# The opening of a decoder step: two groups in turn, first chunk in halves, squares of x on ACT

## The chip, the cores and the metric

The kernel runs on one NeuronCore of a Trainium2 chip. What counts is the device time of one execution in microseconds. PE is TensorE, DVE is VectorE, ACT is ScalarE, POOL is GpSimd, SP is SyncE, whose queue here only issues DMAs. All times below are microseconds from the start of the span unless marked otherwise.

## What is computed

One layer of a hybrid decoder for 256 prompt tokens and 8 decode tokens (264 columns in all), in f32:

```python
h = rms_norm(x, g_pre_mix)                       # D_MODEL = 2048
z = h @ w_in                                     # 17 groups of 256 columns
qa, ka, va, qb, kb, vb = split(z)                # rope on the first 16 of 64 dims of q and k
o_a = sink_normalise(banded(qa, ka, va, 128))    # 16 heads over 2 kv heads
o_b = merge(dilated(qb, kb, vb, w, d) for w, d in ((128, 1), (512, 4), (2048, 16)))
x += rms_norm(concat(rms_norm(o_a), rms_norm(o_b)) @ w_out, g_post_mix)
h = rms_norm(x, g_pre_ffn)                       # D_FF = 5632
y = (gelu(dwconv3(h @ w_gate)) * (h @ w_up)) @ w_down
x += rms_norm(y, g_post_ffn)
```

## The kernel before

All matrices are streamed as chunks of 128x1024 f32 (512 KB, `CH`) through a ring of four slots (`RING`). Chunk n goes through five hands: SP loads it into `raw` as soon as DVE has finished with the chunk four before it (`lo_ready`); ACT casts it to fp32r, `wh` (L390, `hi_ready`); DVE subtracts, `wl = raw - wh` (L627, `lo_ready`); PE multiplies (`gemm`, `weights_used`). A product is three matmuls of 264 columns, `wh*hh`, `wh*hl` and `wl*hh` (L1061 to L1063, `mm3`), where `hh` and `hl` are the high and low parts of x times its gain. A chunk holds four k-tiles of 128 rows by 256 columns, so it is 4 x 2 x 3 = 24 matmuls. A group of 256 output columns of `w_in` takes four chunks, one for each quarter of x; groups alternate between PSUM banks 0, 1 and 2, 3.

The opening: SP issues the small part of `par` (gains), then x in four quarters (4 k-tiles, 528 KB each) alternating with the four chunks of group 0, then the rest of `par`, `ident`, `tab` (masks and cosines, 808 KB), and from chunk 4 on one chunk for each that DVE frees. ACT makes four `hh` (L520) per quarter of x and one cast; DVE makes the `hl` (L786), with its weight operations among them; POOL squares x in four operations of 128x1056 into `xsq` (L999).

After that the order of each engine is a table, `PLAN`: `PLAN[n]` lists the stages that follow chunk n. Each engine walks it in the same way, so DVE and ACT work on their part of the stage behind their operation on chunk n+2 or n+3. The stages that matter here are "ss" (PE sums the squares, L1081), "ss2" (PE sums over partitions, L1100; ACT takes the root, L403; DVE the reciprocal `rB`, L695, and multiplies the cosine tables by it), "evac" of a group (DVE rotates and scales PSUM into q, k or v), "vtr" and "vdec" (PE transposes v), "S" (scores, L1134 and L1136), "R" (DVE scales the exponentials) and "T" (PE transposes them). The row norm 1/rms is applied only at evacuation, so group 0 can be multiplied before it is known, but not evacuated.

Of the kernel before, what the change touches and what calls it, by code (L numbers as in the profile page):

```python
# [178 lines left out]
def build(nc, d):  # L179

    ctx = ExitStack()
    with ctx:
# [158 lines left out]
        def _(sp):  # L341
# [8 lines left out]
            sp.dma_start(xT[:, 0:4], d["x"][:, 0:4]).then_inc(x_landed[0], 16)  # L350
            load(chunk(0, 0, 4, 0), d["w_in"][GROUPS[0][2], 0])
            for c in range(1, 4):
                sp.dma_start(xT[:, 4 * c:4 * c + 4], d["x"][:, 4 * c:4 * c + 4]).then_inc(x_landed[c], 16)
                load(chunk(0, 0, 4, c), d["w_in"][GROUPS[0][2], c])
# [1 line left out]
            sp.dma_start(ident[:], d["ident"]).then_inc(tab_landed, 16)
            sp.dma_start(tab[:], d["tab"]).then_inc(tab_landed, 16)
            for n in range(4, N_IN):
                load(chunk(n, 0, 4, 0), d["w_in"][GROUPS[n // 4][2], n % 4])
# [21 lines left out]
        def _(act):  # L381
# [133 lines left out]
            line.do(nc.scalar.activation(small[:, 100:101], eps[:], ACT.Copy))  # L515
            act.wait_ge(gains_landed, 16)
            for j in range(MT):
                if j % 4 == 0:
                    act.wait_ge(x_landed[j // 4], 16)
                nc.scalar.activation(hh[:, j], xT[:, j], ACT.Copy,  # L520
                                     scale=par[:, C_GPM + j:C_GPM + j + 1]).then_inc(xh_ready, 1)
                if j in (3, 7, 11):
                    split(chunk(0, 0, 4, j // 4))
# [95 lines left out]
        def _(dve):  # L619
# [163 lines left out]
            for j in range(MT):  # L783
# [4 lines left out]
                if j in (3, 7):  # L788
                    split(chunk(0, 0, 4, j // 4))
# [689 lines left out]
```

## Time and profile before

| | us |
|---|---|
| median of 3 runs | 1202.35 (1202.26 to 1202.55) |
| the profiled execution | 1202.52 |
| its span | 1200.7 |
| mean granted clock of TensorE | 0.992 |
| PE busy | 1164.7 (97%) |
| DVE busy | 704.1 (59%) |
| ACT busy | 551.3 (46%) |
| POOL busy | 115.2 (10%) |

A row of a timeline reads: start, duration, engine, line, operation, output and inputs, shapes, count, and in brackets how long the engine was idle before it and what ended that. Durations of matmuls overlap, so for PE the distance from start to start is what one costs. The span begins 1.8 us short of the whole time; the difference lies around it.

### The profile page before, as it was taken

To read this page: it belongs to the slowest core of one execution; us is meant where nothing else is said; L and a number is where in the kernel's file an instruction comes from. 1 tells how busy PE (TensorE), PEld (TensorE's weight loads), DVE (VectorE), ACT (ScalarE), POOL (GpSimd) and SP (SyncE) were. 2 spreads that over 40 slices of the span, in tenths; PEclk is the share of its full clock that TensorE was granted. 3 is DMA by queue.
4 is the path that set the end of the run, shared out by engine and by line. 5 is a ranking of instruction groups with operands and counts; after the bars stand their busy time and mean duration, and the time that the engine had idled before them with its cause. 6 is when DMAs were issued, how large, how long until landed. Compare 5 with 4: busy or idle time off the path is not lost.

```text
span 1200.7 us, 25500 instructions
## 1 busy us (share of the span) xinstructions
PE 1164.7 (97%) x9921; PEld 1132.3 (94%) x9921; DVE 704.1 (59%) x1049; ACT 551.3 (46%) x855; POOL 115.2 (10%) x167
## 2 busy tenths in 40 slices
PE   5999999999999799999999999999999999999995
PEld 4999898989899799999999999999999999999995
DVE  6786665576475866656565655656565444454445
ACT  5445555565455654445344444444444433343331
POOL 3100111111002001001001100100010000020001
PEclk9999999999999899999999999999999999999998
DMA  7555786777556346464555555554555655555551
GB/s 290 172 174 158 257 245 231 232 226 249 183 159 179 116 136 202 158 208 160 190 166 184 179 170 194 173 190 156 196 170 193 193 179 185 176 178 184 181 157 73
DMA packets 59042, 222.21 MB, mean 185 GB/s; under 512 B 7017, under 2 KB 7217, under 8 KB 56881
## 3 DMA queue, kind: packets, MB, share of 16 engines
q1 hardware_dynamic: 54720, 196.58, 50.4%
q0 software_dynamic: 4272, 24.94, 6.3%
q8 instruction: 35, 0.57, 0.2%
q14 instruction: 15, 0.11, 0.0%
HBM read 216.45 MB, written 5.00 MB: 184 GB/s over the span
## 4 chain that ended last, share of the span: by engine, by line
PE 93%; DVE 4%; DMA 1%; ACT 1%; issue 0%; POOL 0%; SPq 0%; DVEq 0%; ACTq 0%
PE ps L1061 29%; PE ps L1062 29%; PE ps L1063 29%; DVE hl L786 1%; PE ps L1227 1%; PE ps L1145 1%; DMA Vk<-in_vb 1%; DVE wl L627 1%; PE ps L1208 1%; PE ps L1136 1%; PE ps L1134 1%; PE ps L1163 0%; PE ps L1081 0%; DVE yT L905 0%; DMA xT<-in_x 0%
## 5 line engine op out<-in xcount | busy, mean ns | idle before, releaser
L1061 PE MATMUL ps<-hh,wh 128*128 128x264 f32 x2080 | 601.2, 289 | 19.2 <-DVE wl L627 13.5
L1063 PE MATMUL ps<-hh,wl 128*128 128x264 f32 x2080 | 594.2, 286 | 0.0
L1062 PE MATMUL ps<-hl,wh 128*128 128x264 f32 x1952 | 558.8, 286 | 0.0
L627 DVE TENSOR_TENSOR wl<-raw,wh 128x1024 fp32r<-128x1024 f32 x364 | 439.4, 1224 | 187.7 <-ACT wh L390 187.3
L390 ACT CAST wh<-raw 128x1024 fp32r<-128x1024 f32 x364 | 375.7, 1045 | 282.7 <-PE ps L1063 272.0
L1061 PEld LDWEIGHTS ps<-hh,wh 128*128 128x128 f32 x2080 | 395.1, 190 | 31.3 <-issue 16.9
L1063 PEld LDWEIGHTS ps<-hh,wl 128*128 128x128 f32 x2080 | 394.1, 189 | 0.0
L1062 PEld LDWEIGHTS ps<-hl,wh 128*128 128x128 f32 x1952 | 369.8, 189 | 0.1
L1062 PE MATMUL ps<-gl,wh 128*128 (+1 forms) x704 | 200.4, 285 | 0.0
L1061 PE MATMUL ps<-gh,wh 128*128 (+1 forms) x704 | 200.1, 284 | 0.0
L1063 PE MATMUL ps<-gh,wl 128*128 (+1 forms) x704 | 199.5, 283 | 0.0
L1061 PEld LDWEIGHTS ps<-gh,wh 128*128 128x128 f32 x704 | 132.5, 188 | 0.9 <-issue 0.9
L1062 PEld LDWEIGHTS ps<-gl,wh 128*128 128x128 f32 x704 | 132.6, 188 | 0.0
L1063 PEld LDWEIGHTS ps<-gh,wl 128*128 128x128 f32 x704 | 132.4, 188 | 0.0
L1027 POOL COPY co<-U 128x4 f32 (+1 forms) x22 | 21.2, 964 | 423.4 <-DVE U L841 423.4
L840 DVE TENSOR_TENSOR U<-ps,rB 128x512 f32<-128x512 f32 x22 | 15.2, 691 | 73.2 <-PE ps L1063 73.2
L865 DVE TENSOR_TENSOR up<-ps,rB 128x528 f32<-128x528 f32 x21 | 14.9, 707 | 67.8 <-PE ps L1063 67.8
L576 ACT ACTIVATE cv<-U,par 128x280 f32<-128x280 f32 x44 | 25.0, 617 | 63.5 <-DVE U L841 63.5
L586 ACT CAST gh<-up 128x528 f32 (+1 forms) x22 | 14.0, 634 | 73.0 <-DVE up L868 72.9
L850 DVE SCALAR_TENSOR_TENSOR cv<-U,par,cv 128x280 f32<-128x280 f32 x88 | 41.0, 506 | 9.9 <-ACT cv L576 6.9
L1061 PE MATMUL ps<-oBh,wh 128*128 128x264 f32 x128 | 37.6, 294 | 0.0
L1062 PE MATMUL ps<-hh,wh 128*128 128x264 f32 x128 | 36.5, 285 | 0.0
(224 smaller groups left out, 830.7 us busy)
## 6 DMA issues: line engine op xcount, KB each, us to landing
raw<-in_w_gate SPq DMA_DIRECT2D x88, 512.0 KB, 3.7
raw<-in_w_up SPq DMA_DIRECT2D x88, 512.0 KB, 4.6
raw<-in_w_down SPq DMA_DIRECT2D x88, 512.0 KB, 4.3
raw<-in_w_in SPq DMA_DIRECT2D x68, 512.0 KB, 4.8
raw<-in_w_out SPq DMA_DIRECT2D x32, 512.0 KB, 3.8
Kt<-in_kb POOLq DMA_DIRECT2D x8, 1284.0 KB, 6.2
Vk<-in_vb POOLq DMA_DIRECT2D x8, 1024.0 KB, 7.5
xT<-in_x SPq DMA_DIRECT2D x4, 528.0 KB, 6.6
```

The lines of the kernel that those rows point to most:

```text
L390: nc.scalar.copy(wh[:, slot], raw[:, slot]).then_inc(hi_ready, 1)
L576: nc.scalar.activation(cv[:, k], U[:, k, 0:NU - 2], ACT.Identity, scale=par[:, bass.ds(i * 2 + (C_CW + k), 1)], bias=par[:, bass.ds(i * 2 ...
L586: nc.scalar.copy(gh[:, bass.ds(i * 2, 2)], up[:]).then_inc(gh_ready, 1)
L627: V.tensor_tensor(wl[:, slot], raw[:, slot], wh[:, slot].bitcast(F32), ALU.subtract).then_inc(lo_ready, 1)
L786: V.scalar_tensor_tensor(hl[:, j], xT[:, j], par[:, C_GPM + j:C_GPM + j + 1], hh[:, j].bitcast(F32), ALU.mult, ALU.subtract).then_inc(xl_r ...
L840: line.do(V.tensor_tensor(U[:, :, 2:2 + SEQ], ps[:, g:g + 2, 0:SEQ], wide(rB[:, 0:SEQ]), ALU.mult))
L850: ins = V.scalar_tensor_tensor(cv[:, k], U[:, k, tap:tap + NU - 2], par[:, bass.ds(i * 2 + (C_CW + FT * tap + k), 1)], cv[:, k], ALU.mult, ...
L865: V.tensor_tensor(up[:], ps[:, 2:4, 0:TOK], wide(rB[:]), ALU.mult).then_inc(up_taken, 1)
L1027: line.do(G.tensor_copy(co[:, bass.ds(i * 2, 2), 0:2], U[:, :, SEQ:SEQ + 2]))
L1061: nc.tensor.matmul(out, a, x, start=start, stop=False)
L1062: nc.tensor.matmul(out, a, xl, start=False, stop=False)
L1063: return nc.tensor.matmul(out, b, x, start=False, stop=stop)
```

## The change

Nothing but the first ten chunks and what stands between them is written differently.

- Order of chunks: groups 0 and 1 are multiplied in turn, a quarter of x at a time (`part_in`): chunk 0 is group 0 quarter 0, chunk 1 group 1 quarter 0, chunk 2 group 0 quarter 1, and so on. Group 0 ends with chunk 6, group 1 with chunk 7.
- The first chunk and the first quarter of x are loaded in halves; the first chunk is cast and subtracted in halves too (`half_landed`, `half_hi`, `half_lo`).
- `xsq` is made by ACT with Square (in four operations), not by POOL. ACT loads the Sqrt table at the start.
- `hl` of x is made by DVE just ahead of the quarter that needs it.
- "ss" stands at chunk 4 (was 2), "ss2" at 5 (3), "evac" of group 0 at 7 (4), of group 1 at 8 (8), "vtr" at 8 (5), "vdec" at 9 (6), "aload" (loads of cache A by POOL) at 9 (8). All later stages keep their places.
- The cosine tables are loaded after chunk 5, `ident` and the masks after chunk 7, the rest of `par` after chunk 9. The sinks stand in the first part of `par`.
- In the evacuation of group 0 the value product comes before the second rotation product and signals `kv_taken`; the first matmul of group 2 waits for it.
- PE multiplies `ones` by `ones` 13 times (128x128, f32) at the start, into a bank that is not yet used.

```diff
-C_SINK = C_ST + FT * 16
-T_MA, T_MB, T_COS, T_SIN, T_MD = 0, 384, 768, 768 + TOK, 768 + 2 * TOK
+T_COS, T_SIN, T_MA, T_MB, T_MD = 0, TOK, 2 * TOK, 2 * TOK + 384, 2 * TOK + 768
+FIRST = 8
+WARM = 13
+X_PARTS = ((0, 2), (2, 4), (4, 8), (8, 12), (12, 16))
+def part_in(n):
+    return (n % 2, n // 2) if n < FIRST else (n // 4, n % 4)
 def group_end(gi):
+    if gi < 2:
+        return FIRST - 1 + gi
...
-    add(2, "ss")
-    add(3, "ss2")
+    add(4, "ss")
+    add(5, "ss2")
...
             sp.dma_start(par[:, 0:C_CW], d["par"][:, 0:C_CW]).then_inc(gains_landed, 16)
...
+            load_x(0)
+            sp.dma_start(raw[:, 0, 0:CH // 2], w0[:, 0:CH // 2]).then_inc(half_landed, 16)
+            load_x(1)
+            sp.dma_start(raw[:, 0, CH // 2:CH], w0[:, CH // 2:CH]).then_inc(raw_landed[0], 16)
+            load_in(1)
+            load_x(2)
+            load_in(2)
+            load_x(3)
+            load_in(3)
+            load_x(4)
+            load_in(4)
+            load_in(5)
+            sp.dma_start(tab[:, 0:2 * TOK], d["tab"][:, 0:2 * TOK]).then_inc(angles_landed, 16)
+            load_in(6)
+            load_in(7)
+            sp.dma_start(ident[:], d["ident"]).then_inc(tab_landed, 16)
+            sp.dma_start(tab[:, 2 * TOK:], d["tab"][:, 2 * TOK:]).then_inc(tab_landed, 16)
+            load_in(8)
+            load_in(9)
             sp.dma_start(par[:, C_CW:], d["par"][:, C_CW:]).then_inc(par_landed, 16)
...
-            line.do(nc.scalar.activation(small[:, 100:101], eps[:], ACT.Copy))
+            line.do(nc.scalar.activation(small[:, 100:101], eps[:], ACT.Sqrt))
...
+            high(0)
+            act.wait_ge(half_landed, 16)
+            nc.scalar.copy(wh[:, 0, 0:CH // 2], raw[:, 0, 0:CH // 2]).then_inc(half_hi, 1)
+            high(1)
+            act.wait_ge(raw_landed[0], 16)
+            nc.scalar.copy(wh[:, 0, CH // 2:CH], raw[:, 0, CH // 2:CH]).then_inc(hi_ready, 1)
+            split(chunk(0, 0, 4, 1))
+            high(2)
+            split(chunk(0, 0, 4, 2))
+            square_x(0)
+            square_x(1)
             for n in range(N_ATT):
                 split(chunk(0, 0, 4, n + 3))
+                if n == 0:
+                    high(3)
+                    square_x(2)
+                elif n == 1:
+                    high(4)
+                    square_x(3)
...
-                line.step(V.stream_shuffle(sh[:, 0:n], src, SWAP))
+                line.do(V.stream_shuffle(sh[:, 0:n], src, SWAP))
+                if n == 1:
+                    V.tensor_tensor(vT[:, 0], ps[:, 1, 0:TOK], rB[:], ALU.mult).then_inc(kv_taken, 1)
+                line.need(line.n)
...
-            for c in range(4):
-                pool.wait_ge(x_landed[c], 16)
-                G.tensor_tensor(xsq[:, 4 * c:4 * c + 4], xT[:, 4 * c:4 * c + 4], xT[:, 4 * c:4 * c + 4],
-                                ALU.mult).then_inc(xsq_ready, 1)
...
+            pe.wait_ge(const_ready, 2)
+            for k in range(WARM):
+                nc.tensor.matmul(ps[:, 6, 0:P], ones[:], ones[:], start=True, stop=True)
             for n in range(N_ATT):
                 if n < N_IN:
-                    gi, c = n // 4, n % 4
-                    if c == 0 and gi >= 2:
+                    gi, c = part_in(n)
+                    if c == 0 and gi == 2:
+                        pe.wait_ge(kv_taken, 1)
+                    elif c == 0 and gi > 2:
                         pe.wait_ge(evac_done, gi - 1)
                     gemm(chunk(0, 0, 4, n), 2 * (gi % 2), hh, hl, 4 * c, c == 0, c == 3,
-                         xl_ready if gi == 0 else None)
+                         xl_ready if gi < 2 else None)
```

DVE at the start of the program, before (L786 makes a low part of x, L627 one of weights; "x3" means three alike in a row):

```order
L786 SCALAR_TENSOR_TENSOR hl<-xT,par,hh 128x264 [waits xh_ready,gains_landed]
L786 SCALAR_TENSOR_TENSOR hl<-xT,par,hh 128x264 [waits xh_ready] x3
L627 TENSOR_TENSOR wl<-raw,wh 128x1024 [waits hi_ready]
L786 SCALAR_TENSOR_TENSOR hl<-xT,par,hh 128x264 [waits xh_ready] x4
L627 TENSOR_TENSOR wl<-raw,wh 128x1024 [waits hi_ready]
L786 SCALAR_TENSOR_TENSOR hl<-xT,par,hh 128x264 [waits xh_ready] x8
L627 TENSOR_TENSOR wl<-raw,wh 128x1024 [waits hi_ready] x4
```

The same place of DVE now (L844 the low parts of x, L849 and L853 the halves of chunk 0, L681 the later chunks):

```order
L844 SCALAR_TENSOR_TENSOR hl<-xT,par,hh 128x264 [waits xh_ready]
L849 TENSOR_TENSOR wl<-raw,wh 128x512 [waits half_hi]
L844 SCALAR_TENSOR_TENSOR hl<-xT,par,hh 128x264 [waits xh_ready] x2
L853 TENSOR_TENSOR wl<-raw,wh 128x512 [waits hi_ready]
L681 TENSOR_TENSOR wl<-raw,wh 128x1024 [waits hi_ready]
L844 SCALAR_TENSOR_TENSOR hl<-xT,par,hh 128x264 [waits xh_ready] x4
L681 TENSOR_TENSOR wl<-raw,wh 128x1024 [waits hi_ready] x2
L844 SCALAR_TENSOR_TENSOR hl<-xT,par,hh 128x264 [waits xh_ready] x4
L681 TENSOR_TENSOR wl<-raw,wh 128x1024 [waits hi_ready]
L844 SCALAR_TENSOR_TENSOR hl<-xT,par,hh 128x264 [waits xh_ready] x4
L681 TENSOR_TENSOR wl<-raw,wh 128x1024 [waits hi_ready] x3
```

The low parts of the third and fourth quarter of x, which stood ahead of chunk 2's weights, now stand behind those of chunks 3 and 4.

ACT now, from the second half of chunk 0 (L566) to chunk 5 (L555 a high part of x, L559 a square, L424 a cast of weights):

```order
L566 CAST wh<-raw 128x512 [waits raw_landed0]
L424 CAST wh<-raw 128x1024 [waits raw_landed1]
L555 ACTIVATE hh<-xT,par 128x264 [waits x_landed2]
L555 ACTIVATE hh<-xT,par 128x264 x3
L424 CAST wh<-raw 128x1024 [waits raw_landed2]
L559 ACTIVATE xsq<-xT 128x1056 x2
L424 CAST wh<-raw 128x1024 [waits raw_landed3]
L555 ACTIVATE hh<-xT,par 128x264 [waits x_landed3]
L555 ACTIVATE hh<-xT,par 128x264 x3
L559 ACTIVATE xsq<-xT 128x1056
L424 CAST wh<-raw 128x1024 [waits weights_used,raw_landed0]
```

Before, ACT had only high parts and casts there; the squares are new on it.

DVE around the reciprocal and the first evacuation, before (L694 to L698 the reciprocal and its tables, L636 to L652 rotation and value product of group 0):

```order
L694 TENSOR_SCALAR small<-par 128x17 [waits tab_landed,par_landed,misc_ready,misc_free]
L695 RECIPROCAL rB<-rms 128x264
L697 TENSOR_TENSOR tab<-tab,rB 128x264 [waits dve_line]
L698 TENSOR_TENSOR tab<-tab,rB 128x264
L627 TENSOR_TENSOR wl<-raw,wh 128x1024 [waits hi_ready,dve_line]
L636 SCALAR_TENSOR_TENSOR r<-ps,tab 128x264 [waits weights_used]
L637 STREAM_SHUFFLE sh<-ps 128x264
L638 SCALAR_TENSOR_TENSOR sh<-sh,tab 128x264 [waits dve_line]
L639 TENSOR_TENSOR kA<-r,sh 128x264 [waits dve_line]
L652 TENSOR_TENSOR vT<-ps,rB 128x264 [waits dve_line]
```

And now:

```order
L749 TENSOR_SCALAR small<-par 128x17 [waits angles_landed,misc_ready,misc_free]
L750 RECIPROCAL rB<-rms 128x264
L752 TENSOR_TENSOR tab<-tab,rB 128x264 [waits dve_line]
L753 TENSOR_TENSOR tab<-tab,rB 128x264
L681 TENSOR_TENSOR wl<-raw,wh 128x1024 [waits hi_ready,dve_line]
L681 TENSOR_TENSOR wl<-raw,wh 128x1024 [waits hi_ready]
L690 SCALAR_TENSOR_TENSOR r<-ps,tab 128x264 [waits weights_used]
L691 STREAM_SHUFFLE sh<-ps 128x264
L693 TENSOR_TENSOR vT<-ps,rB 128x264
L695 SCALAR_TENSOR_TENSOR sh<-sh,tab 128x264 [waits dve_line]
L696 TENSOR_TENSOR kA<-r,sh 128x264 [waits dve_line]
```

Two weight operations now stand between the tables and the evacuation, where one stood, and the value product has moved up behind the shuffle.

## Rows read from the trace of the kernel before

**Rows 1.** The page's chain that ended last, share of the span by engine.

```profile
PE 93%; DVE 4%; DMA 1%; ACT 1%; issue 0%; POOL 0%; SPq 0%; DVEq 0%; ACTq 0%
```

**Rows 2.** Waits of PE, whole span: us in total, times, longest.

```profile
PE ps L1061 <- DVE wl L627: 13.5, 3, 11.8
```

**Rows 3.** Timeline of PE: start, duration, line, [idle before and its cause].

```profile
11.82 0.59 PE L1061 MATMUL ps<-hh,wh 128*128 128x264 f32 x1 [11.82 <-DVE wl L627]
...
17.05 0.42 PE L1063 MATMUL ps<-hh,wl 128*128 128x264 f32 x1
17.95 0.39 PE L1061 MATMUL ps<-hh,wh 128*128 128x264 f32 x1 [0.48 <-DVE wl L627]
...
22.32 0.39 PE L1061 MATMUL ps<-hh,wh 128*128 128x264 f32 x1 [1.18 <-DVE wl L627]
...
25.44 1.99 PE L1081 MATMUL ps<-xsq,ones 128*32 128x264 f32 x32
...
38.85 0.44 PE L1115 MATMUL ps<-ident,vT 128*128 128x128 f32 x2 [1.97 <-DVE kdup L656]
...
42.08 0.37 PE L1061 MATMUL ps<-hh,wh 128*128 128x264 f32 x1
...
50.84 0.29 PE L1063 MATMUL ps<-hh,wl 128*128 128x264 f32 x1
51.05 0.49 PE L1134 MATMUL ps<-kdup,qs 64*128 64x128 f32 x4
...
403.94 0.56 PE L1061 MATMUL ps<-hh,wh 128*128 128x264 f32 x1 [5.75 <-DVE hl L814]
```

**Rows 4.** Timeline of DVE from 6 to 21 us, pieces of several windows.

```profile
6.07 4.56 DVE L786 SCALAR_TENSOR_TENSOR hl<-xT,par,hh 128x264 fp32r<-128x264 f32 x4 [5.02 <-ACT hh L520]
...
11.69 2.17 DVE L786 SCALAR_TENSOR_TENSOR hl<-xT,par,hh 128x264 fp32r<-128x264 f32 x1
...
15.88 0.88 DVE L786 SCALAR_TENSOR_TENSOR hl<-xT,par,hh 128x264 fp32r<-128x264 f32 x2
...
17.82 3.31 DVE L786 SCALAR_TENSOR_TENSOR hl<-xT,par,hh 128x264 fp32r<-128x264 f32 x8
```

**Rows 5.** Timeline of POOL: the first square, the third, third and fourth together.

```profile
5.41 1.95 POOL L999 TENSOR_TENSOR xsq<-xT 128x1056 f32<-128x1056 f32 x1 [4.07 <-DMA xT<-in_x]
...
10.55 3.03 POOL L999 TENSOR_TENSOR xsq<-xT 128x1056 f32<-128x1056 f32 x1 [0.61 <-DMA xT<-in_x]
...
10.55 5.12 POOL L999 TENSOR_TENSOR xsq<-xT 128x1056 f32<-128x1056 f32 x2 [0.61 <-DMA xT<-in_x]
```

**Rows 6.** ACT's groups by line: count | busy us, mean ns | idle before.

```profile
L390 ACT CAST wh<-raw 128x1024 fp32r<-128x1024 f32 x364 | 375.7, 1045 | 282.7 <-PE ps L1063 272.0 <-DMA raw<-in_w_in 9.9 <-ACT ge L596 0.3
...
L495 ACT ACTIVATE sq<-oT 128x1056 f32<-128x1056 f32 x4 | 4.3, 1084 | 0.1
```

**Rows 7.** The chain in order of time: start, us, what.

```profile
1.20 4.14 DMA xT<-in_x
...
51.12 0.42 PE ps L1134 x4
```

**Rows 8.** The page's DMA issues: count, KB each, us to landing (0 to 60 us).

```profile
par<-in_par SPq DMA_DIRECT2D x1, 40.0 KB, 1.8
```

**Rows 9.** Windows: engines busy (count), granted clock, DMA share, GB/s; the second PE alone.

```profile
20.00:25.00 5.00, 3.82 (x32) 3.61 (x31) 5.00 (x7) 1.04 (x1) 0.00 (x0) 1.00 0.42 136
...
405.00:410.00 5.00, 5.00 (x25) 0.51 0.28 81
```

**Rows 10.** Timeline of DVE: start and end of the reciprocal block, and of an evacuation.

```profile
31.55 0.17 DVE L694 TENSOR_SCALAR small<-par 128x17 f32<-128x17 f32 x1 [5.88 <-ACT rms L403]
...
34.28 1.22 DVE L627 TENSOR_TENSOR wl<-raw,wh 128x1024 fp32r<-128x1024 f32 x1
...
45.29 0.71 DVE L636 SCALAR_TENSOR_TENSOR r<-ps,tab 128x528 f32<-128x528 f32 x1 [0.47 <-PE ps L1063]
...
48.75 1.23 DVE L627 TENSOR_TENSOR wl<-raw,wh 128x1024 fp32r<-128x1024 f32 x1
```

More of the change, by code:

```diff
@@ L349, in _, with load_x, load_in @@
             sp.dma_start(par[:, 0:C_CW], d["par"][:, 0:C_CW]).then_inc(gains_landed, 16)
[L350 to L354, printed above, removed]
+            def load_x(c):
+                k0, k1 = X_PARTS[c]
+                sp.dma_start(xT[:, k0:k1], d["x"][:, k0:k1]).then_inc(x_landed[c], 16)
+            def load_in(n):
+                g, c = part_in(n)
+                load(chunk(n, 0, 4, 0), d["w_in"][GROUPS[g][2], c])
+            w0 = d["w_in"][GROUPS[0][2], 0]
+            load_x(0)
[17 more added lines that the diff above has]
+            load_in(9)
             sp.dma_start(par[:, C_CW:], d["par"][:, C_CW:]).then_inc(par_landed, 16)
[L356 to L359, printed above, removed]
+            for n in range(10, N_IN):
+                load_in(n)
             with sp.Fori(0, (N_OUTA + N_OUTB) // 4) as i:
@@ L514, in _, with high, square_x @@
             act.wait_ge(const_ready, 1)
-            line.do(nc.scalar.activation(small[:, 100:101], eps[:], ACT.Copy))
+            line.do(nc.scalar.activation(small[:, 100:101], eps[:], ACT.Sqrt))
             act.wait_ge(gains_landed, 16)
[L517 to L523, printed above, removed]
+            def high(c):
+                act.wait_ge(x_landed[c], 16)
+                for j in range(*X_PARTS[c]):
+                    nc.scalar.activation(hh[:, j], xT[:, j], ACT.Copy,
+                                         scale=par[:, C_GPM + j:C_GPM + j + 1]).then_inc(xh_ready, 1)
+            def square_x(q):
+                nc.scalar.activation(xsq[:, 4 * q:4 * q + 4], xT[:, 4 * q:4 * q + 4], ACT.Square).then_inc(xsq_ready, 1)
+            high(0)
[9 more added lines that the diff above has]
+            square_x(1)
             for n in range(N_ATT):
                 split(chunk(0, 0, 4, n + 3))
+                if n == 0:
[4 more added lines that the diff above has]
+                    square_x(3)
                 for s in PLAN[n]:
@@ L782, in _, with low_x @@
             dve.wait_ge(gains_landed, 16)
-            for j in range(MT):
-                dve.wait_ge(xh_ready, j + 1)
-                V.scalar_tensor_tensor(hl[:, j], xT[:, j], par[:, C_GPM + j:C_GPM + j + 1],
-                                       hh[:, j].bitcast(F32), ALU.mult, ALU.subtract).then_inc(xl_ready, 1)
-                if j in (3, 7):
-                    split(chunk(0, 0, 4, j // 4))
+            def low_x(c):
+                for j in range(*X_PARTS[c]):
+                    dve.wait_ge(xh_ready, j + 1)
+                    V.scalar_tensor_tensor(hl[:, j], xT[:, j], par[:, C_GPM + j:C_GPM + j + 1],
+                                           hh[:, j].bitcast(F32), ALU.mult, ALU.subtract).then_inc(xl_ready, 1)
+            low_x(0)
+            dve.wait_ge(half_hi, 1)
+            V.tensor_tensor(wl[:, 0, 0:CH // 2], raw[:, 0, 0:CH // 2], wh[:, 0, 0:CH // 2].bitcast(F32),
+                            ALU.subtract).then_inc(half_lo, 1)
+            low_x(1)
+            dve.wait_ge(hi_ready, 1)
+            V.tensor_tensor(wl[:, 0, CH // 2:CH], raw[:, 0, CH // 2:CH], wh[:, 0, CH // 2:CH].bitcast(F32),
+                            ALU.subtract).then_inc(lo_ready, 1)
+            split(chunk(0, 0, 4, 1))
+            low_x(2)
             for n in range(N_ATT):
                 split(chunk(0, 0, 4, n + 2))
+                if n == 1:
+                    low_x(3)
+                elif n == 2:
+                    low_x(4)
                 for s in PLAN[n]:
@@ L1071, in gemm @@
                         pe.wait_ge(split, kt0 + k + 1)
+                    if isinstance(n, int) and n == 0 and k == 2:
+                        pe.wait_ge(lo_ready, 1)
                     for m in range(2):
```

40 lines of the change are left out of this document (25 added, 15 removed).

## The prediction

> **What bounds the kernel now.** First the page's chain of work that ended last: PE holds 93% of it [rows 1]. So only time in which PE stands, or runs slowly, can be won. The table of waits for PE says what it stands for: 13.5 us for DVE's low parts of the weights, 11.8 of it at the very start [rows 2]. Then I read PE's opening as a timeline.
>
> PE's rows [rows 3] give a ledger. It starts at 11.82. The 24 matmuls of the first chunk start 0.227 us apart (11.82 to 17.05), while 72 matmuls from 42.08 to 50.84 start 0.1234 apart. These are the 1.2 and the 2.4 GHz level (264 columns in 0.22 and 0.11), and a fast chunk takes 2.96 us; the first takes 5.3, so 2.3 more. Then PE stands 0.48 and 1.18 us for low parts of weights and 1.97 for the copies of the keys `kdup` (the brackets of the rows). Sum: 11.82 + 2.3 + 0.48 + 1.18 + 1.97 = 17.75 us before the first scores matmul (L1134) at 51.05. The work up to there is ten chunks of 2.96, 1.92 for the sums of squares, 0.46 for the one sum over `rms` and about 0.4 for three transposes: 32.4. That leaves 0.9 us, a quarter or so for each restart. After 51.05 the waits of PE sum to under 1 us up to the middle stall, which ends at 403.94: what is won up to the first scores matmul is won for good.
>
> Why PE starts late: DVE needs 4.56 us for four low parts of x and, from 11.69 to 16.76, 5.07 for four more, while the last eight take 3.31, 0.40 apart [rows 4]. POOL squares x in the same stretch [rows 5]. The fifth low part starts at 11.69 and takes 2.17 us, to 13.86, which is when POOL's third square (10.55 to 13.58) has ended; and that square took 3.03 us where the first took 1.95, with a DVE weight operation (1.21 us) inside it. Each waits for the other as a whole. The seventh and eighth low parts, from 15.88, start when POOL has ended (15.67) and are 0.40 apart while loads still land. So it is POOL, not the landing data, that holds DVE up. The Trainium skill, "SBUF — State Buffer", section "SBUF: two separate sides", says the same in general: VectorE and GpSimd take a shared port pair as a lock for a whole instruction, and DMA has ports of its own; by that rule rival C below has no ground.
>
> **The change, part by part.**
>
> *Squares to ACT.* DVE loses the blocking: 4.56 + 5.07 - 2 x 1.62 = 6.4 us [rows 4]. ACT gets four squares of 128x1056; such a square elsewhere takes 1.09 us [rows 6], so 4 x 1.0 = 4.0 us of ACT's queue. ACT becomes the engine that sets the pace of the opening: 16 high parts x 0.41, eight casts x 0.93 and 4.0 make 18 us for eight chunks, against PE's 8 x 2.96 = 23.7. The squares stand ahead of the casts of chunks 3, 4 and 5, which I follow below.
>
> *First loads halved.* The first quarter of x, 528 KB, landed at 5.34 [rows 7]. Thereafter the queue moves 1040 KB (a quarter of x and a chunk) in the time from one landing of x to the next: POOL's third square starts on landing, at 10.55, two landings later, so 2.6 us each, 0.0025 us per KB. Half of x's quarter should land 264 KB earlier, at 4.7. Bounds: the small gains load (par, 40 KB) lands 1.8 us after its issue at 0.76 [rows 8], which with 0.44 for the later issue and 0.65 for 264 KB is 3.65; the upper end is 5.34, no gain from smaller pieces. I take 4.7, as it is from the same transfer. Then half a chunk at 5.3, x at 6.0, the other half at 6.6, chunk 1 at 7.9, x[4:8] at 9.2, chunk 2 at 10.4, x[8:12] at 11.7, chunk 3 at 13.0, x[12:16] at 14.2.
>
> *PE's start.* ACT: two high parts from 4.77 (0.41 apart), the half cast from 5.59 to 6.21 (half of 1.04 and 0.1 fixed, [rows 6]). DVE: half a low part from 6.28 to 6.96 (1.21 halved and 0.07). PE at 7.03. It was 11.82.
>
> *PE on ones.* 13 products of 128x128 in f32: two such (L1134) take 0.42 us of the chain at the fast clock [rows 7], so 0.42 each at the slow one, 5.5 us from 1.1 to 6.65. That is before 7.03, so it costs nothing; were it at fast clock all along it would end at 3.9. PE has twice gone from rest to the fast level in this trace: 11.82 to about 17.5, and from 403.94 on, where the granted clock of 405 to 410 is 0.51 [rows 9], so to about 410: 5.7 to 6.1 us each. From 1.1 that is 6.8 to 7.2: I take one step of a chunk (6 matmuls, 0.58 us extra) as slow. The Trainium skill, "TensorE: Matmul & The Clock Gate", section "What's actually happening", calls this transition run-variable, which speaks against counting on it; it is rival B.
>
> *Two groups in turn.* Each quarter of x now feeds two chunks (5.92 us of PE) instead of one. In order of queue: chunk 0 is fed by 8.4, chunk 1 by 10.2, chunk 2 by 13.2, chunk 3 by 16.1 (ACT: cast 2 at 10.86, two squares to 13.8, cast 3 to 14.8); PE wants them at 7.0, 10.6, 13.5, 16.5. Chunk 4: ACT does four high parts, one square and the cast (18.39), DVE ends at 19.67, PE wants it at 19.45: **0.29** us. Chunk 5: lo at 23.2, PE is at the sums until 24.6: nothing. The last low parts of x are done by 21.3, ahead of need.
>
> *Reciprocal and first evacuation.* Squares are summed after the fifth chunk (22.7 to 24.6), chunk 5 ends at 27.6, the sum over `rms` at 28.1; ACT's root 28.25 to 28.74. DVE's block from the negation to the second table product is 31.55 to 34.28, 2.7 us [rows 10]: 28.8 to 31.5. Behind it on DVE are two weight operations (2 x 1.14, to 33.8), then product, shuffle and the value product that signals `kv_taken` (1.2 us, to 35.0). This is the wait that the change adds: the first matmul of group 2 needs it, and PE is there at 33.96: **1.1** us. The rest of that evacuation (2.3), one weight operation and the next evacuation (45.29 to 48.75, 3.5 us, [rows 10]) end at 41.9; PE arrives for the first scores at 41.42: **0.6**. The old wait for `kdup` is gone: the transposes of values stand at 38.0, and the keys are copied by 37.3.
>
> *Tables, ident and the rest of par later.* 1.3 MB or 3.3 us of queue. They leave the place ahead of raw chunk 4, which landed at 18.9 and lands now at about 15.5, and go between chunks 5 and 10, where the DMA engines were busy for 0.42 of their time from 20 to 25 [rows 9]. Need: cosines at 28.8, masks at 42. Both are issued before the chunk that waits for lo 5, near 20. Cost nothing, cover over 10 us. What SP waits for in between is a weight slot, as before.
>
> **Sum.** After: 7.03 + 0.58 + 0.29 + 1.1 + 0.6 = 9.6 us of waits and slow clock, plus 32.4 of work is 42.0 for the first scores matmul. Before: 51.05. Gain 9.05 us. The profiled execution was 1202.52 (span 1200.7, 1.8 around it), 0.17 above the median, so I subtract from the median: 1202.35 - 9.05 = **1193.3**. Own range 1191.8 to 1195.0: loads at 3.65 give at most 0.4 (the products on ones end at 6.65), loads at 5.34 cost 0.6, squares and signals slower by a tenth cost 0.5; and the slow stretch behind the middle stall, 3.0 us dearer than at fast clock, may come out by a third longer or shorter, 1.0.
>
> **Rivals.** *B, the products on ones don't bring the clock.* For: they end 0.4 us before the first data. Against: both rises took no longer than these run. Then PE is slow for 6.1 us from 7.03: 3.05 instead of 0.58, less the 0.29 wait that it swallows: 2.2 us, 1195.5. *C, DVE stays slow.* If landing data or ACT beside it and not POOL held DVE up, 16 low parts at 1.14 (4.56/4) instead of 0.40 add 11.8 us to its queue; half of it, 6, falls on PE in waits for chunks 0, 2, 4 and 5: 1199.3. Against: the two at 0.40 while loads land. *D, slower: the clock never rises in the opening.* PE is starved in short pieces, and while it is slow it loses half of the time: the gain is gone when (T - 7.03)/2 = 9.05 + 0.58 + 0.29, the clock still low at T = 27 us; with eight slow chunks the loss is 8 x 2.96 - 0.9 = 22.8 and the time 1216. Against: gaps of 0.48 and 1.18 us did not bring it down [rows 3]. *E, given back later.* The masks, cache loads by POOL and a raw load that ACT waited 5.4 us for at 51.8 meet in another phase, and 3 to 6 us return as PE waits: about 1197.5. Against: from 51 us PE hardly waits. *F, more than told:* 1191 or less, if DVE's queue is shorter than priced at 28 to 42 us (1.7 us) and the middle stall's clock helps too.
>
> **Chances.** Forecast 0.62, B 0.18, C 0.04, D 0.03, E 0.07, F 0.06. The range 1191.4 to 1196.6 takes in the forecast and B and little of E. A difference of 0.2% (2.4 us) is about what a measurement tells from none: faster 0.94, same 0.03, slower 0.03.
>
> **What would show it.** Right: PE's first real matmul at 7.0 (4.8 us gained), spacing 0.12 within a microsecond of it; low parts 0.40 apart; ACT never over 0.5 us late for a chunk; waits of about 1.1 for the value product and 0.6 ahead of the first scores; first scores at 42.0. Wrong: low parts still over 1 us (C), spacing 0.22 beyond 8 us (B) or beyond 27 (D), new PE waits behind 51 us (E).

## The result, and the profile after

The changed kernel takes 1194.49 us (median of 5 runs, 1192.60 to 1196.51) against 1202.35 before: ratio 0.9935, 95% interval 0.9923 to 0.9946, 7.9 us faster. The forecast was 1193.3, its range 1191.4 to 1196.6. The profiled execution took 1196.02 (span 1194.2), 6.50 less than that of before. It is the second highest of its five, which matters below.

PE's waits over the whole span, to be held against [rows 2] (us in total, times, longest):

```profile
PE ps L1130 <- DVE hl L886: 5.8, 1, 5.8
PE ps L1301 <- DMA Vk<-in_vb: 2.2, 1, 2.2
PE ps L1331 <- DVE ones L838: 1.1, 1, 1.1
...
PE ps L1130 <- DVE wl L853: 0.9, 1, 0.9
PE ps L1130 <- DVE vT L693: 0.9, 1, 0.9
PE ps L1130 <- DVE wl L681: 0.7, 2, 0.4
...
PE ps L1208 <- DVE QselA L724: 0.2, 1, 0.2
```

The 13.5 us for low parts of weights have become 1.6 (L853 and L681), and the 1.97 for `kdup` is gone. The 5.8 is the middle stall, there before and after. New are the value product (L693), `QselA` and, far from anything the change wrote, 2.2 us for the loads of `Vk`.

PE in the opening, as [rows 3] (L1331 the products on ones, L1155 the squares, L1208 the first scores):

```profile
1.10 5.92 PE L1331 MATMUL ps<-ones 128*128 128x128 f32 x26 [1.10 <-DVE ones L838]
6.67 0.57 PE L1130 MATMUL ps<-hh,wh 128*128 128x264 f32 x1
7.03 0.38 PE L1131 MATMUL ps<-hl,wh 128*128 128x264 f32 x1
7.25 0.28 PE L1132 MATMUL ps<-hh,wl 128*128 128x264 f32 x1
...
8.34 0.28 PE L1132 MATMUL ps<-hh,wl 128*128 128x264 f32 x1
9.49 0.36 PE L1130 MATMUL ps<-hh,wh 128*128 128x264 f32 x1 [0.87 <-DVE wl L853]
9.69 0.28 PE L1131 MATMUL ps<-hl,wh 128*128 128x264 f32 x1
...
11.58 0.39 PE L1130 MATMUL ps<-hh,wh 128*128 128x264 f32 x1 [0.40 <-DVE wl L681]
...
24.05 2.00 PE L1155 MATMUL ps<-xsq,ones 128*32 128x264 f32 x32
...
36.31 0.39 PE L1130 MATMUL ps<-hh,wh 128*128 128x264 f32 x1 [0.85 <-DVE vT L693]
...
43.03 0.49 PE L1208 MATMUL ps<-kdup,qs 64*128 64x128 f32 x4 [0.24 <-DVE QselA L724]
```

Real work starts at 6.67 instead of 11.82 and is at the fast level after two matmuls (from 7.25 on they start 0.12 apart). It then waits 0.87 us for the second half of chunk 0 and 0.40 for chunk 1. The first scores matmul starts at 43.03, not at the forecast 42.0; it was 51.05, so 8.02 us are gained up to there. The rows also show what a restart costs beyond its bracket: the last matmul before the wait lasts 0.28 us where the next would have started 0.12 behind it, and the first two behind the wait start 0.20 apart instead of 0.12. By these rows that is about 0.2 us for each restart.

Why the second half is late stands in ACT's timeline (L555 high parts of x, L563 and L566 the half casts, L424 the cast of chunk 1):

```profile
4.08 0.92 ACT L555 ACTIVATE hh<-xT,par 128x264 fp32r<-128x264 f32 x2 [1.84 <-DMA xT<-in_x]
5.20 0.62 ACT L563 CAST wh<-raw 128x512 fp32r<-128x512 f32 x1 [0.20 <-DMA raw<-in_w_in]
6.05 0.92 ACT L555 ACTIVATE hh<-xT,par 128x264 fp32r<-128x264 f32 x2 [0.24 <-DMA xT<-in_x]
8.00 0.62 ACT L566 CAST wh<-raw 128x512 fp32r<-128x512 f32 x1 [1.02 <-DMA raw<-in_w_in]
9.22 1.05 ACT L424 CAST wh<-raw 128x1024 fp32r<-128x1024 f32 x1 [0.60 <-DMA raw<-in_w_in]
```

ACT waits for data each time. The first half of x is there by 4.08 (forecast 4.7), the second half of the chunk only at 8.0 (6.6), chunk 1 at 9.2 (7.9). What the DMA engines moved in these microseconds (stretch, length, then granted clock, DMA share, GB/s), in after:

```profile
4.00:5.00 1.00, 1.00 0.87 298
5.00:6.00 1.00, 1.00 0.97 198
6.00:7.00 1.00, 1.00 0.88 295
```

and in before:

```profile
5.00:6.00 1.00, 1.00 1.03 422
6.00:7.00 1.00, 1.00 1.04 425
```

From 5 to 6 us the engines are nearly as busy as before and move less than half as much in this profile. The figure varies: over all eight profiles of a kernel with these halved loads it is 198 to 315 GB/s from 5 to 6 us and 264 to 382 from 6 to 7; over the six with whole loads it is 401 to 434 and 407 to 425.

The gain of 8.02 us is still whole when POOL issues the last load of `Vk`. POOL in after, then in before:

```profile
302.67 0.57 POOL L1059 DMA_DIRECT2D Vk<-in_vb  x1 [8.51 <-PE ps L1301]
```

```profile
310.69 0.57 POOL L987 DMA_DIRECT2D Vk<-in_vb  x1 [8.51 <-PE ps L1227]
```

It isn't whole behind it. PE at that load's first use, after and then before:

```profile
314.95 1.53 PE L1301 MATMUL ps<-Vk,pT 128*32 128x128 f32 x48 [2.16 <-DMA Vk<-in_vb]
```

```profile
321.19 1.53 PE L1227 MATMUL ps<-Vk,pT 128*32 128x128 f32 x48 [0.37 <-DMA Vk<-in_vb]
```

From the issue to where PE wants the data there are 10.1 us in both (312.79 - 302.67 and 320.82 - 310.69). The load and its signal took 10.5 us in before and 12.3 in after, so 1.8 us went back. The restart behind the middle stall is at 397.70 against 403.94, 6.24 earlier, and the whole is 6.50 shorter.

### The profile page after: what moved, and what is told of

Read it like the earlier page. It is cut to its first block, busy times and chain, and to the rows that moved or that the text cites. A ratio compares the mean times of both kernels' runs of the same rounds, so it can differ in the third digit from the quotient of the medians.

```text
span 1194.2 us, 25575 instructions
## 1 busy us (share of the span) xinstructions
PE 1168.1 (98%) x9947; PEld 1135.4 (95%) x9947; DVE 698.4 (58%) x1050; ACT 554.4 (46%) x859; POOL 105.8 (9%) x163
## 4 chain that ended last, share of the span: by engine, by line
PE 93%; DVE 3%; DMA 2%; ACT 1%; issue 1%; SPq 0%; POOL 0%; DVEq 0%; ACTq 0%
PE ps L1130 29%; PE ps L1131 29%; PE ps L1132 28%; PE ps L1301 1%; DMA Vk<-in_vb 1%; PE ps L1219 1%; DVE wl L681 1%; PE ps L1282 1%; DMA xT<-in_x 1%; PE ps L1210 1%; PE ps L1208 1%; PE ps L1237 0%; PE ps L1155 0%; DVE yT L977 0%; DVE ps L976 0%
## 5 line engine op out<-in xcount | busy, mean ns | idle before, releaser
L681 DVE TENSOR_TENSOR wl<-raw,wh 128x1024 fp32r<-128x1024 f32 x363 | 438.4, 1225 | 192.2 <-ACT wh L424 191.7
L424 ACT CAST wh<-raw 128x1024 fp32r<-128x1024 f32 x363 | 374.6, 1046 | 275.4 <-PE ps L1132 272.0
```

Of the source, the lines that this page charges most:

```text
L424: nc.scalar.copy(wh[:, slot], raw[:, slot]).then_inc(hi_ready, 1)
L681: V.tensor_tensor(wl[:, slot], raw[:, slot], wh[:, slot].bitcast(F32), ALU.subtract).then_inc(lo_ready, 1)
```

## Experiments

A median stands with its lowest and highest run; ratios are to before. "First scores" is where the first scores matmul starts in the profiled execution (51.05 before, 43.03 after).

**The changed kernel once more.** Theory V says that what varies from run to run is the last `Vk` load; the rival is an opening that varies.

> The changed kernel once more, word for word. Question: what makes its times spread over 4 us (1192.6 to 1196.5) where the kernel before spreads over 0.5. Theory V (the last load of cached values, Vk for head pair 7, lands in a varying time and PE waits for it, 2.16 us in the first profile): the opening is the same to 0.1 us in this profile (first scores matmul at 43.0), the wait of PE for the last Vk is another number, and the whole time follows it, 1192.4 us plus about that wait less 0.4. Rival O (the opening itself varies, through the loads of x and of the first chunk): the first scores matmul moves by a microsecond or more and the wait for Vk stays at 2.2.

1194.72 us (1193.02 to 1195.92), ratio 0.9939 [0.9926, 0.9953]. This profiled execution took 1194.72, 1.30 less than the first. From chunk 1 on its opening is the same within 0.1 us. Before that it isn't: PE is on real data at 6.33 instead of 6.67, at the fast level at once, and waits 1.52 us instead of 0.87 for the second half of chunk 0, to 9.56 instead of 9.49. Its wait for `Vk` is half:

```profile
43.12 0.49 PE L1208 MATMUL ps<-kdup,qs 64*128 64x128 f32 x4 [0.30 <-DVE QselA L724]
...
313.96 1.52 PE L1301 MATMUL ps<-Vk,pT 128*32 128x128 f32 x48 [0.95 <-DMA Vk<-in_vb]
...
396.71 0.56 PE L1130 MATMUL ps<-hh,wh 128*128 128x264 f32 x1 [5.75 <-DVE hl L886]
```

The restart is 0.99 earlier: the shorter wait gives 1.2, and the stages up to the load are 0.2 later. The difference of the two profiles is as theory V has it, and the first scores don't move. Its formula for the whole time gives 1192.95 and is 1.8 us too low, as it is for the first profile (1194.16 against 1196.02).

**The last `Vk` load cut down.**

```diff
 def load_V(u):
+    if u == OT - 1:
+        G.dma_start(Vk[:, 0, 0], d["vb"][u, :, 0, 0]).then_inc(Vk_landed, 16)
+        G.dma_start(Vk[0:64, 2, 0], d["vb"][u, 0:64, 2, 0]).then_inc(Vk_landed, 16)
+        return
```

> The changed kernel, in which the last load of cached values (head pair 7) brings 96 KB instead of 1280 KB; the values that PE then multiplies are those of the pair before, so the decode rows of that pair are left wrong. Theory V: PE doesn't wait for Vk, the median is 1202.35 - 8.0 (what the opening has won at the first scores matmul) - 0.4 (the wait of before that goes too) = 1193.9 at the most and the spread falls to under 1 us. Rival O: the median falls by the same 2 us at most, but the spread stays at 3 to 4 us.

1193.26 us (1193.08 to 1193.33), ratio 0.9931 [0.9917, 0.9944]. The wait is gone, and the spread of five runs falls from 2.9 us to 0.25. First scores at 42.88, restart at 395.33, 2.37 before that of the first profile, of which 2.16 is the wait. So in this kernel this load is the cause of the spread, and it costs the median 1.5 us (1194.72 - 1193.26). The same edit in before:

> The kernel before, in which the last load of cached values (head pair 7) brings 96 KB instead of 1280 KB; the decode rows of that pair are left wrong. On the chip of the first runs it spread over 0.5 us, on that of the later ones over 4 (1200.2 to 1204.7). Theory V: there too the spread is the wait for the last Vk; without it the median is 1201.5 to 1202.2 and the spread under 1 us, so the true gain of the change, both without that wait, is 1202 - 1193.3 = 8.5 to 9. Rival: the spread stays, and comes from another load.

Its edit is the same. 1201.76 us (1200.35 to 1202.44, 11 runs), ratio 0.9997 [0.9987, 1.0006]: nothing to be had there. The median is as expected, the spread of 2.1 us is not: in before it isn't this load that makes most of it. With this load out of both, the change is worth 1201.76 - 1193.26 = 8.5 us (two chips, on which before itself differs by 0.2).

**Without the products on ones**, to price rival B.

```diff
-WARM = 13
+WARM = 0
```

> The changed kernel without the 13 products of ones at the start of PE. Theory: PE starts on real data at 6.67 as before, but at the 1.2 GHz level for some 6 us; two and a half chunks take 0.22 a matmul. Three microseconds of slow clock, of which the waits for the second half of chunk 0 and for chunk 1 (0.87 + 0.40) are swallowed and perhaps 0.3 at chunk 4: first scores matmul 1.0 to 2.0 us later, median 1195.5 to 1196.5. Rival (the chunks of the opening are paced by ACT and DVE, so a slow PE costs nothing): under 0.5 us later.

1193.78 us (1193.30 to 1194.31), ratio 0.9935 [0.9921, 0.9948]: not slower than with them. PE:

```profile
6.44 0.56 PE L1130 MATMUL ps<-hh,wh 128*128 128x264 f32 x1 [6.44 <-DVE wl L849]
...
11.64 0.42 PE L1132 MATMUL ps<-hh,wl 128*128 128x264 f32 x1
11.86 0.40 PE L1130 MATMUL ps<-hh,wh 128*128 128x264 f32 x1
...
43.16 0.49 PE L1208 MATMUL ps<-kdup,qs 64*128 64x128 f32 x4 [0.30 <-DVE QselA L724]
```

24 matmuls are 0.22 apart instead of 0.12, 2.4 us of slow clock, and all of it lies where PE otherwise waits for the half chunk, chunk 1 and part of chunk 4 (0.87 + 0.40 + 0.15, and three restarts at some 0.2). First scores are 0.04 us from those of the kernel with them. My expectation of a loss was a miss. The clock did come, as I had forecast, and up to the first scores it is worth nothing. That the median is even 0.9 lower says little: this profile has no wait for `Vk`, where those with the products have 2.16 and 0.95.

**Squares back on POOL**, all else as in after.

```diff
...
-                nc.scalar.activation(xsq[:, 4 * q:4 * q + 4], xT[:, 4 * q:4 * q + 4], ACT.Square).then_inc(xsq_ready, 1)
...
+                G.tensor_tensor(xsq[:, k0:k1], xT[:, k0:k1], xT[:, k0:k1], ALU.mult).then_inc(xsq_ready, 1)
...
```

> The changed kernel with the squares of x back on POOL (four operations of 128x1056, each when its part of x has landed), nothing of them on ACT. Theory (POOL and DVE lock each other out for whole operations that read two inputs from SBUF): low parts of x and weights stretch to 1 to 2 us where a POOL square runs, POOL's squares to 3 us; the DVE queue is up to 6 us longer between 6 and 20 us, but ACT is 4 us shorter; PE's chunks 0 to 4 wait 2 to 4 us more, first scores matmul at 45 to 47. Rival (it is only the number of operations per engine that counts, and the lock was harmless but for the start): first scores at 42 to 43, no slower than the changed kernel.

1199.82 us (1198.52 to 1201.71, 11 runs), ratio 0.9984 [0.9975, 0.9993]. DVE (low parts of x) here and in after, then POOL (squares), then PE:

```profile
11.37 4.91 DVE L844 SCALAR_TENSOR_TENSOR hl<-xT,par,hh 128x264 fp32r<-128x264 f32 x4
```

```profile
11.44 1.70 DVE L844 SCALAR_TENSOR_TENSOR hl<-xT,par,hh 128x264 fp32r<-128x264 f32 x4
```

```profile
10.86 2.23 POOL L1073 TENSOR_TENSOR xsq<-xT 128x1056 f32<-128x1056 f32 x1 [2.55 <-DMA xT<-in_x]
```

```profile
9.75 0.36 PE L1135 MATMUL ps<-hh,wh 128*128 128x264 f32 x1 [1.68 <-DVE wl L853]
...
19.22 0.59 PE L1135 MATMUL ps<-hh,wh 128*128 128x264 f32 x1 [4.70 <-DVE wl L681]
```

Four low parts take 4.91 us beside POOL's squares and 1.70 without them. PE stands 4.70 us for it and comes back slow (0.59 for the first matmul). First scores at 48.71, 1.7 beyond what I expected. So the squares are worth 5.6 us of the opening (48.71 - 43.12) and 5.1 of the time inside this change. Of the 5.6, 4.1 are waits of PE (1.68 + 4.70 against 1.52 + 0.40 + 0.32) and about 1.4 the slow clock behind the long one (matmuls 0.22 apart from 19.61 to 22.47). Without the squares the rest of the change keeps 2.5 us (1202.37 beside it on this chip). Which part of that rest brings them, the two groups in turn, the order of the low parts or the later tables, wasn't tried.

**Before, with only the squares moved to ACT** (they stand behind the cast of chunk 3).

```diff
-                G.tensor_tensor(xsq[:, 4 * c:4 * c + 4], xT[:, 4 * c:4 * c + 4], xT[:, 4 * c:4 * c + 4],
-                                ALU.mult).then_inc(xsq_ready, 1)
...
+                if n == 0:
+                    for q in range(4):
+                        nc.scalar.activation(xsq[:, 4 * q:4 * q + 4], xT[:, 4 * q:4 * q + 4],
+                                             ACT.Square).then_inc(xsq_ready, 1)
```

> The kernel before with one part of the change alone: the squares of x on ACT (four operations of 128x1056, behind the cast of chunk 3), none on POOL. Theory (POOL's squares are what delays DVE): the eight first low parts are 0.40 apart, PE starts at 9.4 to 9.6 instead of 11.82, in spite of no other change; sums of squares at about 21, first scores matmul at 46 to 47 instead of 51.05, the median 4 to 5 us lower, 1197.5 to 1198.5. Rival (it takes the order of loads and groups to win anything): PE starts at 11 or later and the first scores matmul is at 50 or later.

1198.38 us (1197.05 to 1201.40, 11 runs), ratio 0.9972 [0.9962, 0.9981]. PE starts at 8.96 instead of 11.82, the squares are summed at 20.48 and the sum over `rms` starts at 25.44, 5 us earlier. Then the old wait for `kdup` (1.99 us) comes, and behind it the clock is down. PE in stretches of 5 us (length, PE busy, granted clock, DMA share, GB/s), this kernel just behind the wait, which ends at 33.9, and then before, where it ends at 38.85:

```profile
35.00:40.00 5.00, 5.00 (x31) 0.66 0.84 275
```

```profile
35.00:40.00 5.00, 3.03 (x26) 1.00 0.33 105
40.00:45.00 5.00, 5.00 (x44) 1.00 0.94 302
```

Matmuls at 0.22 follow for 3.3 us, and the first scores are at 47.63, not at 46 to 47: 5 us won, 1.5 lost again. The time is 4.0 to 4.3 us less than before's (1202.35, and 1202.68 beside it on this chip). By the medians this one part is about half of the change.

**The first quarter of x and the first chunk in one piece**, the rest as in after.

```diff
-X_PARTS = ((0, 2), (2, 4), (4, 8), (8, 12), (12, 16))
+X_PARTS = ((0, 4), (4, 4), (4, 8), (8, 12), (12, 16))
...
-            sp.dma_start(raw[:, 0, 0:CH // 2], w0[:, 0:CH // 2]).then_inc(half_landed, 16)
...
-            sp.dma_start(raw[:, 0, CH // 2:CH], w0[:, CH // 2:CH]).then_inc(raw_landed[0], 16)
+            sp.dma_start(raw[:, 0], w0).then_inc(raw_landed[0], 16)
...
```

> The changed kernel with the first quarter of x and the first chunk loaded whole, as before (528 and 512 KB); casts and low parts still in halves. Question: is the dip of the loads (about 200 GB/s from 4.9 to 6.2 us, second half of the chunk in ACT's hands at 8.0 where I had it at 6.6) made by the small pieces. Theory P (pieces move more slowly): whole, x lands at 5.3, the chunk at 6.6 to 7.0, PE starts at 8.7 to 9.0 and isn't held at chunk 0's second half; since the third chunk is fed at the same time or 0.5 earlier, the first scores matmul is at 42.5 to 43.0, no later than with halves (43.0 to 43.1). Rival (the halves are worth what they bring at PE's start): first scores 1 to 2 us later.

1193.18 us (1192.86 to 1193.50, 4 runs), ratio 0.9925 [0.9911, 0.9939]. ACT and then PE here (the DMA engines moved 401 GB/s from 5 to 6 us):

```profile
5.42 1.73 ACT L558 ACTIVATE hh<-xT,par 128x264 fp32r<-128x264 f32 x4 [3.18 <-DMA xT<-in_x]
...
8.09 1.04 ACT L425 CAST wh<-raw 128x1024 fp32r<-128x1024 f32 x1
```

```profile
8.44 0.39 PE L1133 MATMUL ps<-hh,wh 128*128 128x264 f32 x1 [1.42 <-DVE wl L852]
...
42.24 0.49 PE L1211 MATMUL ps<-kdup,qs 64*128 64x128 f32 x4 [0.29 <-DVE QselA L727]
```

The quarter of x lands 1.3 us after the half did, but nothing is waited for behind it: chunk 1 is cast from 8.09, not from 9.22. PE starts real work 1.8 us later, doesn't stand again until the value product, and is 0.8 us earlier at the first scores (42.24 against 43.03). Halving costs 0.8 us of the opening; I had counted it as a gain. The median is 1.5 below the changed kernel's second one; part of that is the wait for `Vk`, 0.31 in this profile.

**The sum over `rms` in the middle of chunk 5** instead of behind it, so that ACT's root and DVE's queue start earlier.

```diff
+                    if between is not None and k == between:
+                        stage("ss2")
...
-                         xl_ready if gi < 2 else None)
+                         xl_ready if gi < 2 else None, BETWEEN if n == 5 else None)
...
```

> The changed kernel with the one sum over rms (ss2) between the first and second k-tile of chunk 5 instead of behind it: PE does it 2.2 us earlier, no other edit. Theory D (from the root on, DVE's queue sets the pace: reciprocal block 2.7, two weight operations, value product, evacuations): the block starts at 28.0 instead of 30.1, PE's waits for the value product (0.85) and ahead of the first scores (0.3) go, first scores matmul at 42.0 (1.1 earlier), median 1 us lower, 1193.5, within the spread that the last load of values makes. Rival (other work is late next, the weights of chunks 6 to 9): first scores under 0.4 us earlier.

1192.22 us (1191.21 to 1193.35), ratio 0.9918 [0.9905, 0.9930].

```profile
26.61 0.61 PE L1177 MATMUL ps<-rms,ones 128*128 128x264 f32 x2
...
41.37 0.49 PE L1211 MATMUL ps<-kdup,qs 64*128 64x128 f32 x4
```

It starts at 26.61 (28.98 in after), neither the value product nor `QselA` is waited for, and the first scores are 1.66 us earlier, of which 0.2 is won before the edit acts (the squares are summed from 23.85 instead of 24.05). The rival, that the weights of chunks 6 to 9 would be late next and give back all but 0.4 us, falls. Its complement, the first evacuation ahead of DVE's operation on chunk 9, so that only the value product is early:

```diff
                 if kind == "evac":
-                    evac(*a)
+                    if a[0]:
+                        evac(*a)
...
             for n in range(N_ATT):
+                if n == 7:
+                    evac(0)
                 split(chunk(0, 0, 4, n + 2))
```

> The changed kernel with the first evacuation of DVE ahead of its operation on chunk 9 instead of behind it: the value product that the first matmul of group 2 waits for is 1.14 us earlier, nothing else is shorter. Theory D (DVE's queue from the root to the second evacuation is the path, in whatever order): PE's wait of 0.85 for the value product goes, and the wait ahead of the first scores grows from 0.3 to about 1.1; first scores matmul at the same time as the changed kernel, 43.0 within 0.2, median the same within its spread. Rival (kv_taken itself is what the change costs): first scores 0.85 us earlier, 42.2.

```profile
43.05 0.49 PE L1211 MATMUL ps<-kdup,qs 64*128 64x128 f32 x4 [1.16 <-DVE QselA L724]
```

1194.78 us (1193.29 to 1196.11, 4 runs), ratio 0.9936 [0.9920, 0.9953]. The wait for the value product is gone and the one for `QselA` has grown from 0.24 to 1.16; the first scores don't move (43.05). Between the root and the scores DVE's queue as a whole is the path, and its order alone changes nothing.

**The value stage of the last pair one chunk later**, so that `Vk` has 3 us more.

```diff
-                add(e + at, kind, 2 * t + v)
+                add(e + at + (2 * t + v == OT - 1 and kind in ("bV", "bO")), kind, 2 * t + v)
...
```

> The changed kernel with the value stage of head pair 7 (decode, branch B) and all that hangs on it one chunk later in the plan, 3 us more for its load; nothing else. Theory V: PE doesn't wait for Vk any more, the median is 1193.3 and the spread under 1 us, as in the run that left this load out. Rival: the stages behind it (norm of the second half of the attention, its high and low parts) now come too late for the second half of w_out, and PE waits there instead, 1 to 3 us.

1193.65 us (1192.96 to 1194.39), ratio 0.9928 [0.9916, 0.9941]. No wait for `Vk` is left and none has come instead; restart at 396.06, 1.64 earlier than in the first profile. 1.1 us below the changed kernel's second median. The spread of 1.4 us is more than the 1 us I expected.

**All three** (whole first loads, the sum in the middle of chunk 5, the later value stage).

> A version put together from what the runs showed: the changed kernel with the first quarter of x and the first chunk loaded whole (as the run with whole loads), the one sum over rms behind the first k-tile of chunk 5, and the value stage of head pair 7 one chunk later. If the three gains are independent: first scores matmul at 42.24 - 1.7 = 40.5 us, no wait of PE for Vk, median 1193.2 - 0.3 - 1.7 = 1191.2 and a spread under 1.5 us, faster than both kernels. Rival (they share one path, since whole loads and the early sum both feed the same DVE queue): first scores at 41.2 or later, median 1192 or more.

1191.51 us (1190.64 to 1193.25), ratio 0.9912 [0.9898, 0.9926]: 3 us below the changed kernel. PE at the first scores:

```profile
40.90 0.49 PE L1214 MATMUL ps<-kdup,qs 64*128 64x128 f32 x4
```

43.03 less 0.8 and the 1.45 that the early sum brings by itself would be 40.8, so in the opening the two add up. The median lies between the expectation (1191.2) and the rival's bound (1192). The spread of 2.6 us does not fit: I expected under 1.5, and the profile shows no wait for `Vk`. What makes it isn't known.

**Before once more** (one run).

> The kernel before, word for word, for its profile on this chip. Theory V: where its time is over 1202.5, the excess stands in PE's wait for Vk (0.37 in the first profile); first scores at 51.0 within 0.5. Rival: the opening is as much later as the time is longer.

1202.25 us. PE's restarts in the opening are those of [rows 3] less 0.12 us (11.70, 17.83, 22.20, 38.73), but here the clock fell behind the 1.97 us for `kdup`:

```profile
40.00:45.00 5.00, 5.00 (x32) 0.70 0.85 268
```

```profile
52.45 0.49 PE L1134 MATMUL ps<-kdup,qs 64*128 64x128 f32 x4
```

The granted clock was 1.00 there in the first profile of before, shown above, and the first scores were at 51.05. So the expectation of 51.0 within 0.5 is missed by 0.9 us, and the opening of before is not the same in every run. This profile has no wait for `Vk`; the restart is at 404.85 instead of 403.94, and what follows it is 1.2 us shorter than in the first, so the time isn't longer. That the excess of a long run stands in that wait can't be told from this run, as it wasn't a long one.

## Why the prediction was right, and where it was not

*PE starved by DVE, DVE held up by POOL.* Right, and the largest part: 4.91 us for four low parts beside squares and 1.70 without, 5.6 us of opening. The Trainium skill, "SBUF — State Buffer", section "SBUF: two separate sides", gave this rule, that one engine's instruction locks out the other's as a whole, and the trace agrees.

*PE's start.* 7.03 forecast, 6.67 measured (first loads 0.6 earlier than taken), the slow step 0.3 (0.58).

*The loads.* A mis-sized term. I took one rate, 0.0025 us per KB, from 520 KB pieces for 260 KB ones. The half chunk came at 8.0 instead of 6.6, chunk 1 at 9.2 instead of 7.9. Its price: 0.87 + 0.40 us of waits which stand nowhere in my sum, and with three restarts of 0.2 the sums of squares begin at 24.05 instead of 22.7. The half chunk varies from run to run (ACT casts it at 7.09 in the kernel without the products), chunk 1 hardly (9.22 to 9.35 there and in both profiles of the changed kernel). The whole pieces would have been the better change.

*ACT sets the pace but is never late.* Right: squares took 1.0 each, chunk 4's low part was waited for 0.30 us (0.29).

*DVE from the root to the scores.* The block starts at 30.14 instead of 28.8, late by what the loads cost, and what follows has the forecast lengths. The value product is waited for 0.85 (1.1), `QselA` 0.24 (0.6). They came smaller because PE arrived later too. I had named them as two waits; they are one queue, as the two experiments on it show.

*First scores.* 42.0 forecast, 43.03 measured. The sums of squares are 1.35 late: 1.27 for the two waits and 0.6 for three restarts, less 0.36 for the start and 0.27 for the slow step, with 0.1 left over. DVE's block is 1.34 late in turn, and from it to the scores there are 12.9 us instead of 13.2. Together 1.03.

There is a shorter way to the same 1.03, and it names the term that is missing. The waits and slow clock that I forecast were 9.6 us. Measured they are 6.67 + 0.34 + 0.87 + 0.40 + 0.30 + 0.85 + 0.24 = 9.67, the same sum out of other parts: that the errors of the parts cancel is luck. With 32.4 of work this gives 42.07, and the 0.96 up to 43.03 are the five restarts, 0.2 each. My own ledger of before had read 0.9 us for its restarts, and the sum for after put them at nothing. Three restarts, as I forecast them, would have made it 42.6.

*"What is won up to the first scores matmul is won for good."* This step failed. It is rival E in small, with another place and price than I gave it: I had looked at where PE waits after 51 us, and a 0.37 us wait for `Vk` was there to see. I read its size and not its meaning, that this load has no slack: whatever time it takes more than 10.1 us is PE's at once. Against before it took 1.8 more in the first profile and 0.6 more in the second. It is a load whose time varies in either kernel: from issue to landing the longest piece took 9.6 and 8.1 us in the two profiles of before, 11.3 and 10.2 in the two of the changed kernel. In the one without the products on ones, with nearly the same opening, it took 9.2; PE didn't wait for it, and its restart (395.62) keeps the whole gain. So an earlier phase alone doesn't make the load slow, and what does wasn't found.

*The clock behind the middle stall.* From the restart to the end, with what lies around the span, it is 798.6 us in before, 798.3 in after, 798.0 with the last load cut down and 797.4 in the second profile of before: the 1.0 us of my range was about right. (The terms that I named for my own range add up to 1191.9 to 1195.4, not 1191.8 to 1195.0.)

*Rival B.* I gave it 0.18 and 2.2 us. The clock did come with the products on ones. But the price was wrong: without them PE lost nothing, as it then swallows 0.87 + 0.40 + 0.15 and the restarts, where I had counted 0.29. C is excluded by 0.40 per low part while loads landed, D by the spacing from 7.25 on.

So 1193.3 was 1.2 us too low. The first scores came 1.0 late, and `Vk` cost 1.5 of the median, together more than is missing. The surplus came back behind the scores: with `Vk` cut down the restart is 8.6 us earlier than in before, as the 0.37 us wait of before has gone too, and the time is 9.2 less. That the number came out so near is in part luck.

## What to carry to other kernels

When an engine's rows of one kind come in two durations, look for the engine beside it whose instruction ends where the long one does; moving that work to a third engine was worth more here than all the rest of the change. Ahead of an engine that is fed by others, neither its clock nor smaller first pieces need be worth anything: ask which row the next chunk waits for. And a wait of 0.4 us on a long load is a load without slack: count how long it has from issue to use before calling an earlier gain safe. Last, count the restarts: each wait that a change adds has cost here some 0.2 us beyond the idle time that its row shows.

## What the runs showed of the hardware

Pieces of 256 and 264 KB in turn moved 198 to 315 GB/s from 5 to 6 us and 264 to 382 from 6 to 7 (eight profiles), where pieces of 512 and 528 KB moved 401 to 434 and 407 to 425 (six profiles). In the first profile of the changed kernel the busy share was 0.97 and 0.88, in the one with whole loads 0.98 and 1.04.

The clock fell behind a wait of 2.0 us in two profiles (0.66 from 35 to 40 with the squares on ACT, 0.70 from 40 to 45 in the second of before). It stayed at 1.00 in two others: the first of before, with a wait of 1.97, and before with its last load cut down, with 2.05 and first scores at 50.85. Both falls cost 1.5 us up to the first scores. The Trainium skill, "TensorE: Matmul & The Clock Gate", section "What's actually happening", calls the rise run-variable; these profiles show the same of the fall. In later runs before spread over 1200.2 to 1205.1, wider than its first five (1202.09 to 1202.59), also without its last `Vk` load. The clock behind this wait may be a part of it; it isn't settled. The changed kernel has no such wait, so it can't pay this price, which my forecast, read from a run that didn't pay it, leaves out.

The granted clock misleads in the opening. In the kernel without the products on ones, matmuls stand 0.22 apart up to 11.86, and the record reads full speed all along (PE busy and count, granted clock, DMA share, GB/s):

```profile
9.00:11.00 2.00, 2.00 (x11) 1.00 1.03 423
...
13.00:15.00 2.00, 2.00 (x19) 1.00 1.01 414
```

The count tells it: 11 matmuls in 2 us, then 19 (some records are missing). The distance from start to start is the reading to trust there.
